# First block of a two-block network: norm sums and value transposes between two parts of each filling tile, and the decay's running sums behind the next step's scores

## The reference

```
h = rmsnorm(x, attn_norm_g);  proj = h @ w_in          # gla q,k,v,r ; moba q,k,v ; mem q
g_log = log_sigmoid(gla_lr @ w_gla_gk + b) / 16
cum   = cumsum(g_log within chunks of 64)              # the decay's running sums
q_dec = q * exp(cum);  k_inv = k * exp(-cum);  k_end = k * exp(cum_last - cum)
o_gla = intra-chunk (causal q_dec k_inv^T) v + q_dec @ state   # 4 heads, state carried over 8 chunks
q_b, k_b = rmsnorm per head of moba q, k;  o_moba = softmax(q_b k_b^T / 8 - alibi) v   # 4 heads
q_c, k_c = rmsnorm per head;  o_mem = softmax(q_c k_c^T / 8) v     # 4 heads, 256 memory tokens
x = x + concat(o_gla, o_moba, o_mem) @ w_out
x = x + hierarchical_moe(rmsnorm(x)) ; then the second block
```

## Time and profile before

| | |
|---|---|
| time, median of 3 runs | 1747.68 us (1746.02 to 1751.62) |
| the profiled execution's own time | 1748.58 us |
| its span | 1746.8 us |
| busy: TensorE / VectorE / ScalarE / GpSimd | 1694.1 / 698.7 / 604.7 / 577.6 us |
| mean granted TensorE clock | 0.993 |
| steps 0 to 15 and the tiles up to `w_out` | about 44 to 222 us of the span |

### The profile page before, as it was taken

The page is one execution under the profiler, slowest core; times in us unless marked ns, Lnnn a source line. Parts: engine busy times, 40 slices in busy tenths (PEclk is TensorE's granted clock), DMA queues, the critical chain, the costliest instruction groups (busy, mean ns, idle before and its releaser), DMA issues.

```text
span 1746.8 us, 20029 instructions
## 1 busy us (share of the span) xinstructions
PE 1694.1 (97%) x8132; PEld 1177.0 (67%) x8132; DVE 698.7 (40%) x1121; ACT 604.7 (35%) x785; POOL 577.6 (33%) x279
## 2 busy tenths in 40 slices
PE   8999999999999999999999989999999999999996
PEld 5677765344434444437788867777788888888885
DVE  5774445233333333348651013333344421212146
ACT  5665435101000100124751245554333432323232
POOL 2332134222022202014344435555444343434441
PEclk9999999999999999999999999999999999999998
DMA  5121174899999999983212111112242222222301
GB/s 213 61 85 48 39 280 159 343 419 421 421 420 421 421 421 421 421 329 121 87 59 96 49 49 48 50 49 86 78 175 97 97 96 97 96 97 96 134 12 48
DMA packets 79068, 312.74 MB, mean 179 GB/s; under 512 B 3168, under 2 KB 6656, under 8 KB 54272
## 3 DMA queue, kind: packets, MB, share of 16 engines
q1 hardware_dynamic: 78704, 310.38, 45.6%
q0 software_dynamic: 272, 1.05, 0.2%
HBM read 307.22 MB, written 4.19 MB: 178 GB/s over the span
## 4 chain that ended last, share of the span: by engine, by line
PE 88%; DVE 7%; ACT 3%; issue 1%; POOL 1%; DMA 0%; DVEq 0%; SPq 0%; ACTq 0%
PE ps L905 44%; PE ps L1275 13%; PE ps L955 7%; PE ps L1299 6%; PE ps L1228 4%; PE ps L903 2%; PE ps L1418 2%; PE ps L1244 2%; PE ps L1245 1%; PE ps L1407 1%; PE ps L1455 1%; PE ps L1392 1%; ACT sb_slot L1501 1%; DVE sb_xT L2329 1%; DVE sb_h_low L2048 1%
## 5 line engine op out<-in xcount | busy, mean ns | idle before, releaser
L839 POOL TENSOR_TENSOR sb_w_parts<-sb_slot,sb_w_parts 128x2048 fp32r<-128x2048 f32 x59 | 274.9, 4659 | 379.1 <-ACT sb_w_parts L1501 379.1
L905 PE MATMUL ps<-sb_h_high,sb_w_parts 128*128 128x512 f32 x1120 | 268.4, 392 | 0.0
L905 PEld LDWEIGHTS ps<-sb_h_high,sb_w_parts 128*128 128x128 f32 x1120 | 210.2, 188 | 46.9 <-issue 3.1
L1501 ACT ACTIVATE sb_w_parts<-sb_slot 128x2048 fp32r<-128x2048 f32 x59 | 112.8, 1913 | 195.7 <-PE ps L905 186.7
L1275 PE MATMUL ps<-sb_slot,sb_hT 128*64 128x512 f32 x768 | 171.1, 595 | 0.0
L905 PE MATMUL ps<-sb_hidden_high,sb_w_parts 128*128 128x512 f32 x704 | 165.0, 389 | 0.0
L905 PEld LDWEIGHTS ps<-sb_hidden_high,sb_w_parts 128*128 128x128 f32 x704 | 132.2, 188 | 27.4
L803 POOL TENSOR_TENSOR sb_tile_parts<-sb_slot,sb_tile_parts 128x1024 fp32r<-128x1024 f32 x32 | 78.4, 2449 | 189.8 <-ACT sb_tile_parts L1501 189.8
L905 PE MATMUL ps<-sb_h_low,sb_w_parts 128*128 128x512 f32 x560 | 138.0, 389 | 0.0
L1275 PEld LDWEIGHTS ps<-sb_slot,sb_hT 128*64 128x64 f32 x768 | 53.6, 137 | 106.2 <-issue 106.2
L825 POOL TENSOR_SCALAR sb_chosen<-sb_cst,sb_small 128x256 fp32r<-128x256 f32 x28 | 25.3, 921 | 293.5 <-PE ps L1228 293.5
(11 more groups left out here) (339 smaller groups left out, 2639.9 us busy)
## 6 DMA issues: line engine op xcount, KB each, us to landing
sb_slot<-w_up SPq DMA_DIRECT2D x24, 2048.0 KB, 14.9
sb_slot<-w_gate SPq DMA_DIRECT2D x24, 2048.0 KB, 14.9
sb_slot<-w_down SPq DMA_DIRECT2D x21, 2048.0 KB, 15.8
sb_slot<-w_in SPq DMA_DIRECT2D x14, 2048.0 KB, 7.9
sb_R<-w_down SPq DMA_DIRECT2D x11, 2048.0 KB, 15.3
sb_slot<-tiles SPq DMA_DIRECT2D x32, 512.0 KB, 3.3
sb_R<-w_gate SPq DMA_DIRECT2D x8, 2048.0 KB, 14.4
sb_R<-w_up SPq DMA_DIRECT2D x8, 2048.0 KB, 15.4
```

The source lines that it names most:

```text
L839: nc.gpsimd.tensor_tensor(low, raw_part(g), high.bitcast(F32), ALU.subtract).then_inc(w_low, 1)
L905: ins = nc.tensor.matmul(o, w[:, k, at:at + P], h[:, k, :], start=first, stop=last)
L1501: return nc.scalar.activation(dst, src, f, **kw)
```

## The change

For a step with one filling tile, the tile is now split: its high pass, then the `post` of the tiles of the step before (`middle`), then its low pass. For a step with two, `post` comes between the two tiles. The step `norm_rows` and the evictions now stand behind `post` in the list. The VectorE's part of `decay` becomes a step of its own, `decay_sum`, which comes one or two steps later (in step 3 instead of 2, and in step 6 instead of 4), behind `norm_rows`.

```diff
-    late = {0: ["mem_acc"], 1: ["mem_sum"], 2: [("decay", 0)], 4: [("decay", 1)], 5: [("decay_qk", 0)], 8: [("turn_keys", 0), ("intra", 0)],
+    late = {0: ["mem_acc"], 1: ["mem_sum"], 2: [("decay", 0)], 3: [("decay_sum", 0)], 4: [("decay", 1)], 5: [("decay_qk", 0)], 6: [("decay_sum", 1)], 8: [("turn_keys", 0), ("intra", 0)],
...
+    def middle(i):
+        if i == 0:
+            post("mk", 1)
+        elif fills[i - 1][0] != "gla_out":
+            for f in fills[i - 1]:
+                post(*f)
...
             if fills[i][0] == "gla_out":
                 gla(*fills[i])
+                step("norm_rows", i)
+                middle(i)
             else:
-                for f in fills[i]:
-                    tile(*f)
+                if len(fills[i]) == 1:
+                    split_to(TILES1.index(fills[i][0]) + 1)
+                    step("passes", *fills[i][0])
+                else:
+                    tile(*fills[i][0])
+                middle(i)
+                tile(*fills[i][-1])
                 for f in fills[i]:
                     step("evict", *f)
-            step("norm_rows", i)
-            if i == 0:
-                post("mk", 1)
-            elif fills[i - 1][0] != "gla_out":
-                for f in fills[i - 1]:
-                    post(*f)
+                step("norm_rows", i)
...
-            pending = []
+            pending, begun = [], set()
...
-                if kind == "tile":
+                if kind == "passes":
+                    tile(*arg, range(KD), True, True, ((0, 0), (1, 0)))
+                    begun.add(arg)
+                elif kind == "tile" and arg in begun:
+                    tile(*arg, range(KD), True, True, ((0, 1),))
+                elif kind == "tile":
...
-                elif kind == "decay":
+                elif kind == "decay_sum":
```

## The result

The changed kernel takes 1759.13 us (median of 6 runs, 1755.56 to 1760.19), the kernel before 1746.74 beside it (6 runs, 1745.33 to 1751.62): ratio **1.0061, 95% interval 1.0047 to 1.0075**. It is slower, by about 11 us by the ratio (12.4 by these medians), where +3.7 was forecast, and it lies outside the range. The profiled execution took 1760.16 us, with a span of 1758.3; the one before had 1746.8. The difference of the spans, 11.5 us, is what the traces have to explain.

The account below looks back on a forecast made before the run. The TensorE, busy for 97% of the span, was taken as the bound, so only its idle time and clock counted. Terms 3.1 - 3.5 + 4.6 + 0.9 - 1.2 + 0.6 - 0.8 = +3.7 gave 1751.4 us, range 1745 to 1757.

Parts of the forecast that it names:

- its clock: Step 6, at the wait before `gv0`: half-rate clock costs 0.1 to 1.7 us behind the wait, taken as +0.9.
- step 7: Before `gv1`: the wait for ScalarE's root goes, since `gv1` takes the bank of `gv0`; -1.2 us.
- `gv3`'s bank: Step 12: `gv3` waits for the second half of `intra 1`'s eviction instead of the first; +0.6 us.
- `turn_v gv3`: Step 13: placed between the passes of `r0`, its copy is done when `chunk_state 1` asks; -0.8 us.
- Steps 2 to 4: the stall before `gq0` goes: Later running sums let ScalarE's root come in time, removing a 2.2 us wait and 1.3 of clock; -3.5 us.
- Step 6: a new wait in front of `gv0`: `gv0` needs the bank of `score 6 0`; a 10.6 us chain against 6.0 on the TensorE gives +4.6 us.
- Step 0 and 1: New wait before `rowsum mq1`, its eviction behind `mk1`'s reciprocal; `mem_acc` collides with GpSimd, ending at 63.0; +3.1 us.
- Steps 7, 12 and 13: Root wait before `gv1` goes, -1.2 us; `gv3` waits longer for its bank, +0.6; `turn_v gv3`'s copy wait goes, -0.8.
- The slow one: Step 6: a `decay_qk 0` product collides with GpSimd and clock costs its full 1.7; +6.9 us, 1754.6, chance 0.33.
- The fast one: Both new waits, before `rowsum mq1` and `gv0`, stay away and only old ones go; -5.9 us, 1742, chance 0.07.
- the third: Only the wait before `rowsum mq1` comes; chain into `gv0` shorter by 4.6 us or more; -1.8 us, 1746, chance 0.08.
- The low bound of the sum: All terms together with no collision on the ports and clock costs of 0 and 0.1: +1.2 us.

Follow-up runs that it names:

- sums_late: The kernel before with only the running sums moved behind `norm_rows` of steps 3 and 6; 1742.62 us, ratio 0.9971.
- evict_first: The changed kernel, but with two filling tiles the first tile's eviction stands ahead of the posts; 1759.17 us, ratio 1.0071 against the kernel before.
- step6_old: The changed kernel with step 6 alone in the old order, so `gv0` is job 55 again; 1752.16 us, ratio 1.0032 against the kernel before.
- only_step6: The kernel before with the running sums moved late and the new order in step 6 alone; 1751.97 us, ratio 1.0019.
- warm_gv0: The changed kernel with five spare matmuls into an unused bank in front of `gv0`; 1757.19 us, ratio 1.0058 against the kernel before.
- steps_0_3_5_6_12_old: The changed kernel with steps 0, 3, 5, 6 and 12 in the old order, running sums still late; 1745.21 us, ratio 0.9987 against the kernel before.
- posts_ahead: The kernel before with running sums late and, on VectorE and ScalarE only, posts ahead of evictions and `norm_rows` in every step; 1759.49 us, ratio 1.0064.

## Why the prediction was wrong

The forecast's terms beside the measured ones, from the starts above:

| term | forecast | measured |
|---|---|---|
| steps 0 and 1, to `mem_sum` | +3.1 | +4.1, 0.3 of it an offset |
| steps 2 to 4, to the end of `cq1` | -3.5 | -1.0 |
| step 6, wait before `gv0` | +4.6 | +5.9 |
| its clock | +0.9 | +2.0 |
| step 7 | -1.2 | -1.3 |
| `gv3`'s bank | +0.6 | +0.6 |
| clock behind that wait | not in the sum | +1.5 |
| `turn_v gv3` | -0.8 | -0.6 |
| `r2`'s slow pass of before | not in the sum | -1.5 |
| slow stretch at 782 us | not in the sum | +1.7 |
| sum | +3.7 | +11.4 |

(The measured +5.9 is 11.9 us from the end of `cq1` to `gv0`, less the old 6.0. Of it 5.36 stand in front of `gv0` and 0.83 in front of `values 3`, and an old wait of 0.17 for GpSimd is gone. That the slow passes at `r2` and at 782 us nearly cancel, -1.5 and +1.7, is chance.)

- **"Steps 2 to 4: the stall before `gq0` goes"** is the step that failed: -3.5 us were forecast and -1.0 measured. The stall went, and sums_late shows that its 3.5 us were real. But the prediction asked only whether ScalarE's root would be in time. It did not ask which bank `turn 2` needs, and from whom, once evictions stand behind the posts. A wait of 1.95 us and a high pass of 5.54 us took its place, 3.5 us again; evict_first shows that `gk0`'s eviction was the cause. (The 1.0 us are smaller waits that went, two of them for GpSimd's low parts, 0.17 and 0.34.) The same question had been put to `gv0` and answered rightly. It had to be put to every user of a bank whose last job is a tile.
- **"Step 6: a new wait in front of `gv0`"**: the mechanism was right (step6_old takes it away, only_step6 makes it with nothing else), two sizes were off. The chain was put at 10.6 us and measured 11.9, because `ck1`'s scaling ran into GpSimd's low part (1.86 for 0.48). The prediction looked for such collisions in `mem_acc` and in the products, and not at the scaling. The clock was put at 0.9 us, the middle of 0.1 to 1.7; warm_gv0 shows 2.0, above the upper bound. The estimate had 3.4 us at half clock in mind, partly inside the wait; it was 6.8 us, with 4.4 of them in the high pass.
- **"Step 0 and 1"** was right in kind and nearly in size: a wait of 3.20 us for 3.1, and the second addition of `mem_acc` at 2.85 us beside GpSimd. `mem_acc` ended at 62.9 as forecast (63.0), but the slowed TensorE arrived after it, at 64.0: the clock took 0.9 us from the low pass (2.96 for 2.03) and 0.7 from the spare matmul (1.83 for 1.11), where 0.9 in all was taken.
- **Steps 7, 12 and 13** held within 0.2 us, `gv3`'s 0.6 included. What was left out there is that a wait that grows from 1.24 to 1.85 us can bring a slow pass (5.55 us) that the shorter one did not have. In step6_old the same wait did not bring it.
- **The rivals.** The slow one, +6.9, lay nearest to the result but for another reason: its collision did not happen in the changed kernel, and did in evict_first. The fast one was refuted at both waits; the third, with a shorter chain into `gv0`, was refuted by the 11.9 us.
- **The range** ended at 1757. It priced the clock at the two forecast waits alone; a new slow pass at `gv3` and one in the experts (1.5 and 1.7 us) were not in any of its cases. The low bound of the sum, +1.2, does not come out of the terms either: with no clock in step 0, no collision and 0.1 in step 6 they give +1.7, and "without the collision, -1.2" for the end of `cq1` should be -0.7. Neither moves the forecast.

The question of where the remaining clock stretches come from stays open, as does what exactly in steps 1 to 4 holds the last 2 to 3 us of steps_0_3_5_6_12_old, whose interval just meets that of sums_late. The version that beats both kernels is sums_late, at 0.9971.

## What to carry to other kernels

When work is put between a matmul tile and its eviction, list every later job that uses the bank of that tile and every one whose number shifts, and follow each bank to the engine that frees it; one job checked is not enough. Look also at what stands behind a long instruction in its own queue: here a reciprocal of 1.75 or 3.35 us between two tiles cost nothing until an eviction stood behind it. And when a change does two things, price them apart: here the small move of the running sums was a gain of 0.3%, and the reordering around it lost about 0.9%.

## What the hardware showed beyond that

- **Waits can cost clock, and their length alone does not tell.** In the changed kernel all four waits of about 1.9 us and more (1.85, 1.95, 3.20, 5.36) had the granted clock at half in them or soon behind them; those of 0.8 to 1.3 us had not. But in step6_old the same wait in front of `gv3` is followed by a pass at full speed:

```profile
173.39 4.01 PE L971 MATMUL ps<-sb_h_high,sb_tile_parts 128*128 128x512 f32 x16 [1.85 <-DVE sb_R L2226]
```

  In posts_ahead a wait of 2.26 us in front of `values 3` brought none either (the pass behind it took 3.99), while one of 1.30 in front of `rowsum mq1` did (the spare matmul behind it took 2.05 for 1.10). Where the clock fell, a high pass took 5.2 to 5.9 us for 4.00, and 6.0 to 6.6 behind the waits of 4 to 7 us before `gv0`. Where the 5.36 us were filled with spare matmuls it did not fall.
- **Some slow stretches have nothing in front of them that other traces lack.** `r2`'s pass in the kernel before (5.52 us) has no wait in front of it. A stretch in the experts (782 us in the changed kernel) comes in seven of the thirteen traces, and not in the kernel before or in sums_late, although the same waits of 1.04 and 0.79 us stand ahead of it there. Each moves a span by 1.5 to 1.7 us, so that two traces can differ by that much with no cause in the edit.
- **A low part of GpSimd stretched more kinds of VectorE work than the two-operand addition.** The scaling of 256 columns went from 0.48 us to between 1.77 and 1.86 in the changed kernel. And in sums_late the running sum itself was caught, beside a low part at 87.36 (2.59 us). VectorE's timeline:

```profile
87.72 3.31 DVE L2185 TENSOR_TENSOR_SCAN sb_R<-sb_cst,sb_R 128x512 f32<-128x512 f32 x1
```

  The scan takes 1.23 us where it begins ahead of the low part (91.41 in the changed kernel, with GpSimd at 91.99). There GpSimd is the one that is late: its low part took 2.80 us, where 2.35 to 2.41 is usual. In both cases the one that began second was the late one. The long scan cost nothing in sums_late, since `soft 4` had the room.
